# Latent attention heads: the second rope score pass as two 64-row products into two PSUM banks

## The reference

```
c_q, c_kv, k_pe, gate = split(u @ w_in)             # 256, 128, 64, 1024 columns
q_nope, q_pe = split(rms(c_q) @ w_qup)              # 8 heads of 128 + 64
k_nope, v    = split(rms(c_kv) @ w_kvup)            # 8 heads of 128 + 128
q = concat(q_nope, rope(q_pe));  k = concat(k_nope, rope(k_pe))   # k_pe: one for all heads
s = q @ k.T / sqrt(192)                             # 1024 queries, 256 + 1024 keys
o = softmax(s) @ v
h = h + gt * ((o * silu(gate)) @ w_out)
```

## Time and profile before

| | us |
|---|---|
| median of 3 runs | 2503.21 |
| lowest, highest | 2502.32, 2503.75 |
| the profiled execution: its own time | 2504.19 |
| its span, first to last instruction | 2502.4 |
| TensorE busy | 2457.4 |
| stage of the eight latent heads, about | 1617 to 2057 |

### The profile page before, as it was taken

One profiled execution on the slowest core, in us unless ns is written; L12 is line 12 of the kernel. 1 busy time (PEld: TensorE's weight loads), 2 busy tenths in 40 slices (PEclk: granted clock), 3 DMA queues, 4 the chain that ended last, 5 costly groups with the idle time before them and its releaser, 6 DMA issues.

```text
span 2502.4 us, 33946 instructions
## 1 busy us (share of the span) xinstructions
PE 2457.4 (98%) x12166; PEld 2030.4 (81%) x12166; DVE 1445.7 (58%) x1986; ACT 855.8 (34%) x1281; POOL 978.1 (39%) x1022
## 2 busy tenths in 40 slices
PE   8999999999999999999999999999999999999998
PEld 6777787787887788888888878888998988788886
DVE  7846574735457877777421472377777773633344
ACT  4232222223224554554100242156666661311121
POOL 5343444333444876777444533201000005223242
PEclk9999999999999999999999999999999999999999
DMA  5134243421433233223554211100000002111112
GB/s 181 47 105 156 93 153 117 143 76 51 169 109 110 101 107 128 101 101 120 233 188 156 84 53 34 51 10 10 16 8 8 9 9 69 34 34 34 42 42 76
DMA packets 54421, 210.75 MB, mean 84 GB/s; under 512 B 6420, under 2 KB 7700, under 8 KB 49082
## 3 DMA queue, kind: packets, MB, share of 16 engines
q1 hardware_dynamic: 50340, 194.92, 22.5%
q10 hardware_dynamic: 3990, 14.59, 1.6%
HBM read 173.30 MB, written 38.55 MB: 85 GB/s over the span
## 4 chain that ended last, share of the span: by engine, by line
PE 88%; DVE 7%; ACT 2%; issue 2%; DMA 0%; POOL 0%; DVEq 0%; SPq 0%; ACTq 0%; POOLq 0%
PE PS L749 40%; PE PS L1087 15%; PE PS L1116 10%; PE PS L1373 4%; PE PS L1307 4%; PE PS L1347 3%; PE PS L1313 3%; PE PS L941 1%; PE PS L976 1%; PE PS L1297 1%; PE PS L778 1%; PE PS L842 1%; PE PS L1557 1%; PE PS L967 1%; PE PS L1191 1%
## 5 line engine op out<-in xcount | busy, mean ns | idle before, releaser
L749 PE MATMUL PS<-H,w_hl 128*128 128x512 f32 x4272 | 1003.9, 393 | 9.7 <-DVE H L2306 5.2
L749 PEld LDWEIGHTS PS<-H,w_hl 128*128 128x128 f32 x4272 | 794.3, 188 | 195.1 <-issue 17.4
L694 POOL CAST w_hl<-w_raw 128x1024 fp32r<-128x1024 f32 x138 | 155.6, 1128 | 1340.8 <-PE PS L749 791.6
L675 POOL TENSOR_TENSOR w_hl<-w_raw,w_hl 128x256 fp32r<-128x256 f32 x568 | 517.0, 940 | 11.4
L1087 PE MATMUL PS<-BT,WS 128*128 128x512 f32 x1056 | 247.4, 389 | 1.6 <-DVEq L2776 0.7
L1116 PE MATMUL PS<-FFD,w_hl 128*128 128x512 f32 x1056 | 239.8, 389 | 0.1
L1087 PEld LDWEIGHTS PS<-BT,WS 128*128 128x128 f32 x1056 | 197.9, 188 | 44.5 <-issue 1.4
L1116 PEld LDWEIGHTS PS<-FFD,w_hl 128*128 128x128 f32 x1056 | 198.1, 188 | 41.6 <-DVEq L2634 0.5
L703 POOL TENSOR_TENSOR WS<-w_raw,WS 128x256 fp32r<-128x256 f32 x176 | 181.3, 1055 | 48.6 <-ACT WS L1873 47.5
L1087 PE MATMUL PS<-B,WS 128*128 128x512 f32 x792 | 187.1, 389 | 1.6 <-ACT KEEP L1906 1.6
L1087 PEld LDWEIGHTS PS<-B,WS 128*128 128x128 f32 x792 | 148.5, 188 | 32.8 <-issue 2.0
(11 more groups left out here) (350 smaller groups left out, 3025.6 us busy)
## 6 DMA issues: line engine op xcount, KB each, us to landing
w_raw<-in_units SPq DMA_DIRECT2D x186, 512.0 KB, 3.6
AW<-in_ada SPq DMA_DIRECT2D x48, 512.0 KB, 4.3
ff_part<-FFS SPq DMA_DIRECT2D x20, 1024.0 KB, 4.9
FFD<-ff_part SPq DMA_DIRECT2D x20, 1024.0 KB, 5.8
X<-in_x SPq DMA_DIRECT2D x8, 512.0 KB, 9.2
x_part<-SC SPq DMA_DIRECT2D x8, 512.0 KB, 2.6
X<-x_part SPq DMA_DIRECT2D x4, 1024.0 KB, 8.4
out<-X SPq DMA_DIRECT2D x16, 256.0 KB, 2.3
```

The lines of the kernel that those rows point to most:

```text
L675: ins = pool.tensor_tensor(lo_part[:, part], raw[:, part], hi_part[:, part].bitcast(F32), ALU.subtract)
L694: pool.tensor_copy(hi_part, raw).then_inc(w_hi, 1)
L749: mm = pe.matmul(PS[:, out_at + a:out_at + a + m], w(s, wp, w0 + k), src[:, o:o + m], start=(k == 0 and wp == 0 and xp == 0), stop=(k == k ...
```

## The change

The first rope pass (high parts of the keys) stays as it is, for all three pieces. In the second pass only the piece of 256 keys stays one product over 128 rows. For the two pieces of 512 keys, `rope_low_pair` issues two products of 64 rows each: rows 0 to 63 (high parts of the queries, QPS) against the keys' low parts of piece 0 into the first bank, and rows 64 to 127 against the keys' low parts of piece 1 into the second bank. Rows 64 to 127 of QPS hold low parts, so a new buffer `QPD` holds a copy of the high parts on these rows. The product q_lo·k_lo is left out for these 1024 keys. In `mla_scores` the pair stands between piece 1 and piece 2, in `first_scores` it is the last thing. ACT makes QPD with one more copy in each call of `rope_hi`, ahead of the copy into QPS, and `rope_lo` waits for both.

```diff
+    QPD = at("QPD", T, H_AT + 61440, F32R)
...
-        def rope_scores(t, a, m):
+        def rope_scores(t, a, m, low=False, stop=False):
             base = 1536 * (t % 2)
-            for kp_ in range(2):
-                mm = pe.matmul(PS[:, base + a:base + a + m], QPS[:, t * P:(t + 1) * P],
-                               KPE[:, kp_ * TK + a:kp_ * TK + a + m], start=False, stop=(kp_ == 1))
+            return pe.matmul(PS[:, base + a:base + a + m], QPS[:, t * P:(t + 1) * P],
+                             KPE[:, low * TK + a:low * TK + a + m], start=False, stop=stop)
+
+        def rope_low_pair(t):
+
+            base = 1536 * (t % 2)
+            for n, queries_ in enumerate((QPS, QPD)):
+                rows, a = slice(64 * n, 64 * n + 64), HALF * n
+                mm = pe.matmul(PS[:, base + a:base + a + HALF], queries_[rows, t * P:(t + 1) * P],
+                               KPE[rows, TK + a:TK + a + HALF], start=False, stop=True)
             return mm
...
                 nope_scores(t, a, m)
                 mm = rope_scores(t, a, m)
-            mm.then_inc(sc_done, 1)
+                if a == 512:
+                    rope_low_pair(t)
+            rope_scores(t, 1024, 256, low=True, stop=True).then_inc(sc_done, 1)
...
             for a, m in PIECES:
-                mm = rope_scores(t, a, m)
-            mm.then_inc(sc_done, 1)
+                rope_scores(t, a, m)
+            rope_scores(t, 1024, 256, low=True, stop=True)
+            rope_low_pair(t).then_inc(sc_done, 1)
...
             act.wait_ge(qp_sum, h * 2 + (half + 1))
+            act.activation(QPD[64:128, part], TMP0[0:64, part], ACT.Copy).then_inc(qp_hi, 1)
             act.activation(QPS[0:64, part], TMP0[0:64, part], ACT.Copy).then_inc(qp_hi, 1)
...
-            v.wait_ge(qp_hi, h * 2 + (half + 1))
+            v.wait_ge(qp_hi, h * 4 + 2 * (half + 1))
```

## The result

| | before | changed |
|---|---|---|
| median of 5 runs, us | 2503.75 | 2515.98 |
| lowest, highest | 2502.32, 2506.01 | 2515.31, 2517.11 |
| span of the profiled execution | 2502.4 | 2515.1 |

The ratio is 1.0048 with a 95% interval of 1.0035 to 1.0061: slower by 12.2 us of medians, 8.8 to 15.3 by the interval. Forecast were 2514.4 and +11.2.

A forecast was written before the change was run, and what follows sets the result against it. TensorE was taken to bound the heads. Row switches net of overlap (55 x 0.175 = 9.6 us) plus the copy's stall (1.6 us) gave 11.2 us, moving the median from 2503.2 to 2514.4 us, range 2510 to 2518 (82%).

The forecast's parts named there:

- The bound: Latent heads: TensorE, busy 54.6 of 55 us at full clock, sets the pace except where it waits.
- The overlap: Scores of a tile: the two 64-row products run side by side, 0.01 us apart, gaining 0.215 us a tile.
- The price of the switches: Each tile's scores: going to 64-row products and back costs 0.39 us, by emptying and exposed loads; net +0.175 us.
- rival A: Scores: switches are free and the pair costs one product; 55 tiles gain 0.215 us each, 2493.0 us; chance 4%.
- How many tiles pay: Of 64 tiles 55 pay, 9.6 us; each head's tile 2 and the first head's tile 1 end in waits.
- The copy: ACT's extra copy of 0.54 us delays DVE's low parts and stalls tile 7's transposes: 7 x 0.23 = 1.6 us.
- by how much is the third step late: Tile 7's transposes: DVE's third low-parts step comes 0.23 us late for the seventh transpose.
- just in time: Start of tile 7's transposes: DVE's first low-parts step, delayed by the copy, is ready at 1785.52, needed at 1785.56.
- The sum: Whole kernel: 9.6 + 1.6 = 11.2 us slower, median 2514.4 us.
- B: Switches: the array empties but the pair's weights are loaded beforehand, round trip 0.2 us; +0.8 us, 2504.0; chance 5%.
- C: Scores: fp32r products on 64 rows do not overlap, each tile costs the whole 0.39 us; 2526.3 us; chance 4%.
- D: ACT's copies are not covered: the second half's 0.54 us reaches TensorE in every head; 16.7 us, 2519.9; chance 5%.

The follow-up runs named there:

- same_rows: Changed kernel with both 64-row products on rows 0 to 63, unable to run side by side, without QPD or extra copy: 2525.66 us (1.0085).
- pair_twice: Changed kernel with the pair of 64-row products issued twice in a row between the same two switches: 2529.86 us (1.0103).
- tile2_undone: Changed kernel, but tile 2 of each head does its second rope pass with 128-row products as before: 2515.71 us (1.0050).
- pair_no_copy: Changed kernel without QPD and the extra copy; the second 64-row product takes QPS's low parts instead: 2515.03 us (1.0044).
- copies_only: Changed kernel with its extra copy and order of products, but the pair replaced by the earlier two 128-row products: 2505.46 us (1.0010).
- two_tiles: Changed kernel with the copy moved later and tiles 2, 4, 6 leaving their pair to the next tile; tiles 0, 1 use 128 rows: 2525.73 us (1.0096).
- late_copy: Changed kernel with ACT's copy into QPD moved behind tile 6's high parts (first half) and the latents' copy (second half): 2512.88 us (1.0040).
- two_tiles_dve: two_tiles with DVE doing the odd tile's low parts ahead of the even tile's row maximum: 2532.18 us (1.0117).
- exp_early: Kernel before, with tile 1's exponential ahead of tile 0's third probs_hi step on ACT at a head's start: 2500.47 us (0.9986).

## Why the prediction was right

**The bound.** TensorE sets the pace of the heads; right. The part that is not on it (ACT's copy) reached the time only through TensorE's wait.

**The overlap.** Right: the pair starts together, and same_rows costs one product more in each paying tile.

**The price of the switches.** Right in mechanism and size: 0.39 from the earlier trace rows and 0.42 from the earlier trace rows against 0.40 in the changed kernel's tile and by same_rows. The net came out at 0.16 to 0.17 in place of 0.175, because the overlap gains what a product costs, 0.225 to 0.235, and not 0.215. pair_twice shows that it is paid once a visit, at the switches. That one- and 64-row products of plain float32 priced those of fp32r was the choice that the forecast hung on, and it held. The Trainium skill's TensorEngine Tiling (Array Packing), Key Properties, has the emptying; the runs add that the weights are not loaded across a switch. The Trainium skill's TensorE: Matmul & The Clock Gate, Part 3 (Packing small matmuls), has the overlap, which the traces confirm with 0.01 us of lag and less, and no price for leaving the mode; rival A, made of it alone, would have given 2493.0 and fell.

**How many tiles pay.** Right for tile 2 (tile2_undone). The stage of pair_no_copy is 9.2 us longer than before, where 9.6 was forecast; for 55 tiles that is 0.167 each. Tile 1 of the first head was not tested by itself.

**The copy.** Place and mechanism right, the term too small: 0.33 to 0.35 us a head, 2.3 to 2.5 us for seven, not 1.6. By stage it is 11.7 - 9.2 = 2.5 us, and 2.8 in copies_only. The step "by how much is the third step late" was right with 0.23; left out was that each break in TensorE's stream exposes a load. The first transposes, "just in time" by 0.04 us in the forecast, have an idle loader ahead of them too, waiting for DVE (0.25 us in the changed kernel's row above), and expose 0.055 us.

**The sum.** 9.6 + 1.6 = 11.2 against 9.2 + 2.5 = 11.7 in the stage by the traces, and 12.2 in the medians. The pair's term was 0.4 too large and the copy's 0.9 too small; that the sum is off by only 0.5 is in part luck. The medians could not have shown any of it: their interval is 8.8 to 15.3 us.

**Rivals B to D.** B: fell by the idle loader at both switches. C: fell by same_rows. D: fell. Of the copy only the stall at tile 7's transposes reaches the period; the 0.08 us that copies_only loses at tile 2 vanish in the gap. The uncovered price of 0.54 in every head would have given a period of 55.4 or more in copies_only, and it was 55.00.

## What to carry to other kernels

Two products on different row groups do run as one, but a lone pair between 128-row products pays about 0.40 us for going there and back and gains 0.23. Two pairs in one visit gained 0.06 us in two_tiles, and the waits for the late scores ate many times that: pack at least two pairs into a visit before counting on a gain, and first check that whoever waits for their results can wait. A step added on a helper engine costs by its place in the queue, not by its length: the same copy cost about 2.5 us ahead of what TensorE waits for and nothing behind it. And where a view of waits names one row on a saturated engine, reordering its chain (0.5 us a head here) can be worth more than making the engine's own work cheaper.

## What the hardware showed that was not expected

The granted clock fell at the end of the heads in some executions. In the last head TensorE waits twice (1.1 and 1.5 us) for the low parts of the last tiles. Busy times by stretch of the changed kernel, where the next to last column group gives the clock (columns: us; busy us and count of PE, PEld, DVE, ACT, POOL; clock; DMA share; GB/s):

```profile
2061.00:2066.00 5.00, 3.29 (x26) 2.52 (x24) 3.48 (x8) 4.21 (x9) 0.00 (x0) 1.00 0.00 0
2067.00:2073.00 6.00, 6.00 (x29) 6.00 (x30) 2.45 (x2) 3.75 (x4) 0.00 (x0) 0.50 0.01 3
```

The same two stretches of the kernel before:

```profile
2051.00:2056.00 5.00, 3.18 (x25) 2.41 (x23) 3.44 (x8) 4.22 (x9) 0.00 (x0) 1.00 0.01 2
2057.00:2060.00 3.00, 3.00 (x26) 3.00 (x26) 2.37 (x2) 3.00 (x4) 0.00 (x0) 1.00 0.03 5
```

With nearly the same busy time ahead (3.3 and 3.2 us of 5), TensorE ran at half its clock (1.2 GHz) in one and at full (2.4 GHz) in the other, and the thirty products took 6.5 against 3.9 us. late_copy's trace has the fall as well:

```profile
2064.59 6.59 PE L1388 MATMUL PS<-PT,CKT 128*128 128x256 f32 x30 [1.47 <-DVE PT L3039]
```

So of the changed kernel's profiled span 2.7 us are this. Of the twelve traces four have the fall there: changed, late_copy, two_tiles_dve (6.56 us for the thirty products) and tile2_undone (5.26). All four are among the nine whose heads have 64-row products, and none of the other three (before, copies_only, exp_early) has it. Five of the nine don't have it either, so the pair does not bring it every time; whether it makes the fall more frequent is open, since one execution of each kernel doesn't tell.
